# First mixing stage: one pair of transposes of the keys moved from TensorE to DMA, with the merge on ScalarE, and two scale vectors folded into one column

## The reference

```python
u = rmsnorm(h, mix_norm[l])
qa, ka, va, qb, kb, vb, qi, ki, wi, g = jnp.split(u @ w_in[l], SPLIT_POINTS, axis=-1)
qa = rmsnorm(qa.reshape(B, S, 8, 64), q_norm_dsa[l]);  ka = rmsnorm(..., k_norm_dsa[l])
qb = rmsnorm(qb.reshape(B, S, 8, 64), q_norm_moba[l]); kb = rmsnorm(..., k_norm_moba[l])
out_a = dsa_attention(qa, ka, va, qi, ki, wi, bias_dsa)    # only the 64 best keys of each query
out_b = moba_attention(qb, kb, vb, bias_moba)              # one block of 256: plain causal attention
g_a, g_b = jnp.split(sigmoid(g + b_gate[l]), 2, axis=-1)
h = h + (g_a * (out_a @ w_branch_dsa[l]) + g_b * (out_b @ w_branch_moba[l])) @ w_out[l]
```

## Time and profile before

| | |
|---|---|
| median of 3 runs | 997.86 us |
| the profiled execution | 998.35 us |
| its span, first to last instruction | 996.5 us |
| PE busy | 990.7 us, 99% |
| DVE busy | 689.2 us, 69% |
| ACT busy | 548.2 us, 55% |
| POOL busy | 116.0 us, 12% |
| granted TensorE clock | 1.0 of full speed throughout |

### The profile page before, as it was taken

The page is one execution under the profiler, slowest core; times in us unless marked ns, Lnnn a source line. Parts: engine busy times, 40 slices in busy tenths (PEclk is TensorE's granted clock), DMA queues, the critical chain, the costliest instruction groups (busy, mean ns, idle before and its releaser), DMA issues.

```text
span 996.5 us, 12586 instructions
## 1 busy us (share of the span) xinstructions
PE 990.7 (99%) x4632; PEld 813.2 (82%) x4632; DVE 689.2 (69%) x1010; ACT 548.2 (55%) x752; POOL 116.0 (12%) x109
## 2 busy tenths in 40 slices
PE   8999999999999999999999999999999999999998
PEld 7788888888877788888888888888888888888887
DVE  6756566668987667656566677797689767656663
ACT  7344443576765546444443576768875555443542
POOL 0000000022300000000000041168914000000000
DMA  7987776585444446666666376457556546787761
GB/s 258 283 262 258 234 253 211 185 307 175 147 150 141 169 133 211 227 204 208 220 195 226 127 259 211 141 177 211 148 183 199 205 152 212 227 221 227 223 199 43
DMA packets 159129, 199.87 MB, mean 201 GB/s; under 512 B 49633, under 2 KB 105322, under 8 KB 158954
## 3 DMA queue, kind: packets, MB, share of 16 engines
q1 hardware_dynamic: 159066, 199.24, 62.8%
q10 hardware_dynamic: 16, 0.00, 0.0%
HBM read 182.45 MB, written 5.77 MB: 189 GB/s over the span
## 4 chain that ended last, share of the span: by engine, by line
PE 97%; DVE 1%; DMA 1%; ACT 0%; SPq 0%; issue 0%; POOL 0%; ACTq 0%; DVEq 0%; POOLq 0%
PE bank L1902 23%; PE bank L1904 23%; PE bank L1903 23%; PE bank L2018 7%; PE bank L2019 7%; PE bank L2020 7%; PE bank L1917 1%; PE bank L2069 1%; PE bank L2183 1%; DMA halves_t<-halves 0%; DMA raw<-in_ffn_w_gu 0%; PE bank L2084 0%; PE bank L2071 0%; PE bank L2257 0%; PE bank L2141 0%; PE bank L2304 0%
## 5 line engine op out<-in xcount | busy, mean ns | idle before, releaser
L1902 PE MATMUL bank<-hi,xh 128*128 128x512 f32 (+1 forms) x944 | 375.2, 397 | 0.9 <-DVE lo L1520 0.8
L1904 PE MATMUL bank<-hi,xl 128*128 128x512 f32 (+1 forms) x944 | 367.4, 389 | 0.0
L1903 PE MATMUL bank<-lo,xh 128*128 128x512 f32 (+1 forms) x944 | 366.5, 388 | 0.0
L1277 DVE TENSOR_TENSOR lo<-raw,hi 128x2048 fp32r<-128x2048 f32 (+1 forms) x111 | 253.9, 2289 | 146.3 <-ACT hi L799 146.3
L799 ACT ACTIVATE hi<-raw 128x2048 fp32r<-128x2048 f32 (+1 forms) x114 | 216.5, 1901 | 132.3 <-PE bank L2020 96.9
L1902 PEld LDWEIGHTS bank<-hi,xh 128*128 128x128 f32 x944 | 177.3, 188 | 39.5 <-issue 3.1
L1904 PEld LDWEIGHTS bank<-hi,xl 128*128 128x128 f32 x944 | 177.2, 188 | 37.5
L1903 PEld LDWEIGHTS bank<-lo,xh 128*128 128x128 f32 x944 | 177.6, 188 | 34.2
L1294 DVE TENSOR_TENSOR lo<-raw,hi 128x1024 fp32r<-128x1024 f32 (+1 forms) x108 | 133.2, 1244 | 40.1 <-ACT hi L808 39.2
L2018 PE MATMUL bank<-hi,hh 128*128 128x512 f32 (+1 forms) x306 | 119.3, 390 | 0.4 <-DVE hl L1353 0.4
L2020 PE MATMUL bank<-hi,hl 128*128 128x512 f32 (+1 forms) x306 | 118.7, 388 | 0.0
(11 more groups left out here) (266 smaller groups left out, 963.2 us busy)
## 6 DMA issues: line engine op xcount, KB each, us to landing
raw<-in_w_in SPq DMA_DIRECT2D x48, 1024.0 KB
raw<-in_ffn_w_gu SPq DMA_DIRECT2D x82, 512.0 KB
raw<-in_ffn_w_down SPq DMA_DIRECT2D x22, 1024.0 KB
raw<-in_w_up SPq DMA_DIRECT2D x16, 1024.0 KB
raw<-in_w_down SPq DMA_DIRECT2D x16, 1024.0 KB
raw<-in_w_out SPq DMA_DIRECT2D x8, 1024.0 KB
distance_table<-ftab SPq DMA_DIRECT2D x8, 576.0 KB
raw<-in_w_proj_attn SPq DMA_DIRECT2D x4, 1024.0 KB
```

What stands on the lines that cost most here:

```text
L1277: nc.vector.tensor_tensor(lo[s][:, :, 0:width], raw[s][:, :, 0:width], hi[s][:, :, 0:width].bitcast(F32), ALU.subtract).then_inc(lo_done, 1)
L1902: nc.tensor.matmul(o, sh, wh, start=first and j == 0, stop=False)
L1903: nc.tensor.matmul(o, sh, wl, start=False, stop=False)
L1904: ins = nc.tensor.matmul(o, sl, wh, start=False, stop=last and j == 3)
```

## The change

The keys of group 2 (k_m) are no longer turned by PE. `M1_T` loses its two entries for group 2. Instead ACT writes the two 16-bit planes of `hid[:, t]` at steps 14 and 15; SP issues one DMA transpose for each t, placed in its order behind both loads of group 5 (units 10 and 11) and ahead of unit 12; ACT merges both turned halves into k_m with one instruction at step 17; and PE waits for that merge before the first scores (step 21). The planes and their turned form lie in `gates1[:, 0]`, which holds nothing at that time. The scale by the gain is not applied to k_m any more: a fifth DVE instruction in `constants` multiplies the column for q_m by the one for k_m, and q_m's eviction applies the product. The semaphores of the first feed-forward layer are used on. The pieces below are, in this order: the tables, the two views of gates1, SP's loop behind the two loads of group c, three pieces of ACT's loop (what a step does behind the split, the new instructions, the wait ahead of the eviction to hid), DVE's constants, and PE's first scores.

```diff
-M1_T = {(0, 0): 6, (0, 1): 7, (1, 0): 9, (1, 1): 10, (2, 0): 13, (2, 1): 14,
-        (4, 0): 21, (4, 1): 22, (5, 0): 25, (5, 1): 26}
+M1_T = {(0, 0): 6, (0, 1): 7, (1, 0): 9, (1, 1): 10, (4, 0): 21, (4, 1): 22, (5, 0): 25, (5, 1): 26}
+M1_PLANES = (14, 15)
+M1_MERGE = 17
...
+        m_planes = gates1[:, 0, 0:2 * W].bitcast(U16).rearrange("p (t c) -> p t c", t=NT)
+        m_turned_planes = gates1[:, 0, 2 * W:4 * W].bitcast(U16).rearrange("p (k c) -> p k c", c=SEQ)
...
+                if c == 5:
+                    for t in range(NT):
+                        sp_eng.wait_ge(ffns[0].planes, 2 * (NF1 - 1) + t + 1)
+                        sp_eng.dma_start_transpose(m_turned_planes[:, :, t * P:(t + 1) * P],
+                                                   m_planes[:, t, :]).then_inc(ffns[0].flip[t], 16)
...
-                        dst = {1: q_m, 2: k_m, 4: q_a, 5: k_a}[cc]
-                        g = {1: 2, 2: 3, 4: 0, 5: 1}[cc]
+                        dst = {1: q_m, 4: q_a, 5: k_a}[cc]
+                        g = {1: 2, 4: 0, 5: 1}[cc]
                         if order == 2:
-                            act.wait_ge(cols_done, 3)
+                            act.wait_ge(cols_done, 5)
...
+                if p in M1_PLANES:
+                    tt = M1_PLANES.index(p)
+                    act.wait_ge(m_qn, 2 + tt + 1)
+                    nc.scalar.activation(m_planes[:, tt, :].rearrange("p (s c) -> p s c", s=2),
+                                         hid[:, tt, :].bitcast(U16).rearrange("p (c s) -> p s c", s=2),
+                                         ACT.Copy).then_inc(ffns[0].planes, 1)
+                if p == M1_MERGE:
+                    for tt in range(NT):
+                        act.wait_ge(ffns[0].flip[tt], 16 * NF1)
+                    nc.scalar.activation(k_m[:, :, :].bitcast(U16).rearrange("p k (c s) -> p s k c", s=2),
+                                         m_turned_planes.rearrange("p (s k) c -> p s k c", s=2),
+                                         ACT.Copy).then_inc(ffns[0].merged, 1)
...
-                        if m >= 2:
-
-                            act.wait_ge(m_tr, m + 1)
+                        if c == 2:
+
+                            act.wait_ge(m_tr, 2 + t + 1)
+                        elif c == 4:
+                            act.wait_ge(ffns[0].planes, 2 * (NF1 - 1) + t + 1)
+                        elif c == 5:
+                            act.wait_ge(m_tr, 4 + t + 1)
...
+                dve.wait_ge(cols_done, 4)
+                g = C_GAIN + 2
+                nc.vector.tensor_tensor(cols[:, g:g + 1], cols[:, g:g + 1], cols[:, g + 1:g + 2],
+                                        ALU.mult).then_inc(cols_done, 1)
...
-                        pe.wait_ge(m_trev, 6)
+                        pe.wait_ge(m_trev, 4)
+                        pe.wait_ge(ffns[0].merged, NF1)
                     else:
                         pe.wait_ge(m_l, k)
                     if k == NH:
-                        pe.wait_ge(m_trev, 10)
+                        pe.wait_ge(m_trev, 8)
```

## The result

| | before | after |
|---|---|---|
| median | 997.80 us | 999.63 us |
| span of the profiled execution | 996.5 us | 997.7 us |
| that execution's own time | 998.35 us | 999.50 us |

The ratio is 1.0019, with an interval of 1.0012 to 1.0026: slower by 1.83 us (by the interval 1.2 to 2.6). The forecast was 997.6 in a range of 996.7 to 999.0, so the time lies outside it, by 0.6 us on the slow side. It is 0.18% and thus still within what I had called no change, but that is luck of the bound: the sign was wrong. Of the 16 executions of after one took 5704.57 us, for a reason that nothing here shows; it is left out of the ratio, and without it the median would be 999.60.

What follows compares the result with a forecast made beforehand. PE was taken to bound the kernel (97% of the chain), running little ahead of a saturated VectorE. Transposes -0.96, wait at step 23 +0.56, VectorE's delay +0.1 gave -0.3 us: 997.86 to 997.6, range 996.7 to 999.0.

Steps and rivals of the forecast that it cites:

- the rule of the prediction: PE's gain at step 23 is cut to 0.40 - d: transposes free 0.96 us, 0.56 + d returns as a wait.
- d: VectorE's delay at the head sums of step 18: landing - 243.0, range -0.18 to +1.3 us, passed on to PE.
- Landing: When both DMA transposes, issued behind unit 11's load, have arrived for ScalarE's merge: 243.1, range 242.5 to 244.3.
- rival B: Slower: the merge holds ScalarE's queue at step 17, and VectorE; from landing 243.4 on, +0.9 us at 244.3; chance 0.22.
- The sum: Whole kernel: -0.96 (transposes) + 0.56 (wait at step 23) + 0.1 (VectorE's delay) = -0.3 us, median to 997.6.
- -0.96 for eight transposes: PE at steps 13 and 14: removing two groups of four transposes frees 0.48 us each, up to 0.96 us.
- The cap: PE's scores at step 23 need VectorE's negated maximum, whose 0.40 us of slack limits the gain from the 0.96 freed.
- rival A: Full gain: transposes land by 242 or VectorE's slack at step 23 is larger; -0.96 us, 996.9; chance 0.19.
- SyncE's queue: The two transposes' issue makes unit 12's load late by 0 to 0.2 us, with five us of cover: no price.
- Edits without a price: Extra VectorE multiply in constants, product as q's scale, PE's merge wait at step 21, planes in gates1: no cost.

Runs made afterwards that it cites:

- e8: Changed kernel with the eight transposes put back on PE at steps 13 and 14, result unused: 999.83 against 997.96 us, 1.0018.
- e9: Changed kernel with SyncE holding unit 12's load back until both DMA transposes have landed: 999.56 against 997.96 us, 1.0017.
- e10: Changed kernel with the step 17 merge split into two instructions, one per t, each behind its own landing: 998.48 against 997.96 us, 1.0004.
- e7: Changed kernel with the merge at step 18 instead of 17: 997.76 against 997.96 us, 0.9997.
- e1: Changed kernel with the merge at step 19 instead of 17: 996.79 against 997.74 us, 0.9990.
- e2: Changed kernel with the step 17 merge reading unturned planes, the DMA transposes awaited only at step 21: 996.81 against 997.74 us, 0.9990.
- e3: Changed kernel with no transposes on any engine; ScalarE copies unturned keys to k_m at steps 14 and 15: 996.85 against 997.74 us, 0.9991.
- e4: Changed kernel with both DMA transposes ahead of unit 11's load instead of behind it: 996.93 against 997.74 us, 0.9991.
- e11: e1 with the top-k's last instruction moved from step 21 to 24 and the mask work two steps later: 996.54 against 997.96 us, 0.9985.
- e6: e1 with VectorE taking the logits of heads 1 and 3 one step earlier, with heads 0 and 2: 997.35 against 997.96 us, 0.9994.
- e5: Kernel before with only the folded scale (product of two gains as q's scale, k_m evicted with 1.0): 997.91 against 997.96 us, 1.0000.

## Why the prediction was wrong

The table sets the rule of the prediction, net = d - 0.40 at step 23, beside every run with a wait there (us; the last column against the executions of before taken with the run):

| | H | d | S | net measured | d - 0.41 | median against before |
|---|---|---|---|---|---|---|
| after | 17.43 | +2.44 | 31.12 | +2.03 | +2.03 | +1.83 |
| e8 | 17.48 | +2.49 | 31.18 | +2.09 | +2.08 | +1.87 |
| e9 | 17.35 | +2.36 | 31.04 | +1.95 | +1.95 | +1.60 |
| e10 | 16.09 | +1.10 | 29.79 | +0.70 | +0.69 | +0.52 |
| e7 | 15.64 | +0.65 | 29.34 | +0.25 | +0.24 | -0.20 |
| e1, e2, e3 | 14.73 | -0.26 | 28.41 | -0.68 | -0.67 | -0.95, -0.93, -0.89 |
| e4 | 14.74 | -0.25 | 28.42 | -0.67 | -0.66 | -0.81 |

Point by point:

- *The mechanism and the rule were right.* Landing, then merge, then hi, eviction and square in ScalarE's order, then VectorE without a gap, then PE at step 23. The slack read as 0.46 less 0.06 came out as 0.40 to 0.42 us in nine runs. e7 shows that VectorE carries it.
- *The step that failed is "Landing".* I took 243.1, range 242.5 to 244.3. It came at 236.50 + 7.99 = 244.49, in the clock of before 245.06: 2.0 us behind what I took and 0.8 beyond my end. The second transpose took 8.0 us of its own where the four second halves of the earlier trace rows had taken 4.0 to 5.9. I had used the second halves of the second mixing stage as a bound though they go out 2.4 to 3.7 us behind their load (the prediction says 3.1 to 3.7, which holds for the two slow ones) and this one 1.7. The first halves there, 0.5 us behind their load, took 6.1 to 7.6, and I left them out. I had seen the difference in distance and counted it as a reason against rival B; e4 and e9 show that a load just ahead is what delays them, so it spoke for B. Counted from the load's issue the landing took 9.7 us (244.49 - 234.77), near the 9.0 of the earlier trace rows; the forecast went wrong where it averaged that count, at its median, with the transposes' own delays.
- *The merge was mis-sized too.* 2.54 us measured (2.52 to 2.54 in all runs) against 1.9 taken and 2.1 as the upper bound. Twice the planes' 1.04 is not the price of a copy that writes interleaved 16-bit elements: half of it takes 1.37 (e10). That is +0.64 in d.
- *The sum.* d = 2.0 (landing) + 0.6 (merge) + the 0.1 already taken = 2.7, less 0.26 because neighbours on ScalarE overlap (2.39 from the merge's start to that of hi though it lasts 2.54, 1.88 from there to the eviction though hi lasts 1.99), is 2.44, as measured. With it the rule gives +2.03 instead of -0.3.
- *-0.96 for eight transposes was right*, shown by e11 and by e6 at step 23. The 2.2 us that eight times the 271 ns of one would give are more than twice that. Portions 13 and 14 now take 2.73 and 2.72 us, with no transposes in them.
- *The cap was right*: where the square of step 18 waits for no landing (e1 to e4) the gain in the stage stops at 0.68, which is 0.41 and the 0.26 by which the head sums could come earlier (I had allowed 0.18). That limit is why rival A fails too; its -0.96 in the stage is only to be had with e11's edit. The end times of e1 to e4 (-0.81 to -0.95) are nearly A's price all the same, by the difference that is left open below.
- *SyncE's queue:* unit 12 was 1.06 late instead of 0 to 0.2, as the second issue took 4.42 and not at most 3.47 us. It cost nothing, as said.
- *Edits without a price:* confirmed by e5. *The Trainium skill's rule of transposing DMAs as fast as plain ones* ("Advanced Engine Details and Errata", X-Bar Transpose): landing at 242 by it. The trace does not bear it out, though no run has a plain copy of the same data beside them: alone on the DMA engines the transposes of e4 moved 277 GB/s (236.4 to 237.3), unit 11's load in the kernel before 403 (238.2 to 239.4). That is small beside what decided: e4, where nothing is ahead of them, lands at 236.7 + 2.7 = 239.4, and the 6.9 and 8.0 behind a load are not in the rule.
- *Rival B was the right one* in place, price and point of decision (landing from 243.4 on). I gave it 0.22 up to a landing at 245.4 and +2, and its own arithmetic at 245.06 with a merge of 2.54 gives 2.06 + 0.64 - 0.40 = +2.3 (+2.03 with the overlap). The range ended at its row-bound 244.3; landing and merge both lay beyond the rows that I had used, in the same direction.
- *Not foreseen:* PE's wait of 1.55 us for a bank of the accumulators at step 20. By e7 and e8 it adds nothing; PE would have lost as much three steps later.

Open: why a transpose 1.7 us behind a 1 MB load takes 8.0 us and not 5.9, and what it does in the 1.8 us after its data have moved (e9). The distance to the load may be it: 6.1 to 7.6 us at 0.5, 4.0 to 5.9 at 2.4 to 3.7; but among the latter four the order does not follow the distance, and of it I varied only the sign, in e4. And most changed variants end 0.1 to 0.45 us lower against before than their stamp at step 23 says (last two columns; e11 0.45), also those with the transposes on PE or with none. PE's small waits for lo of other stages add up to anything from 0 to 1.4 us in one profiled run or another, which hides differences of that size; I have not found a cause.

## What to carry to other kernels

A wait placed in an in-order queue costs what stands behind it: at steps 17, 18 and 19 the same merge gave +1.83, -0.20 and -0.95 us against before, so put a wait on a DMA behind what a saturated engine needs next, and count the landing of a transfer behind a load from the load's issue, with rows of a similar distance as the bounds. A saving on the bounding engine counts only up to the slack of the engine that feeds it (0.68 of 0.96 here), and the rest was got by moving work that the bounding engine does not wait for behind what it does (e11). Pulling work forward (e6) lost more one step later than it gained. Where a small transfer and a big load are ready together and the load has slack, send the small one first (e4).

## What the runs showed of the hardware

- Two 256 KB transposing DMAs took 2.7 us each from issue to landing with nothing ahead of them (e4), and 6.9 and 8.0 us when they were issued 0.4 and 1.7 us behind a load of 1 MB (after; 6.8 to 8.5 in all eight runs of this order); the issue of the second held the queue for 4.42 instead of 1.23 to 1.25 us.
- Behind a load such a transpose landed 1.8 us after the DMA engines had moved their last data (e9: 242.7 and 244.5), with nothing ahead some 0.5 us after it (e4).
- A ScalarE copy of 16-bit elements took 1.04 us at 128x1024 when it read them interleaved and wrote them in runs (planes) and 1.37 when it read them in runs and wrote them interleaved (e10's merges); 2.54 at 128x2048, where an fp32 split of as many elements takes 1.91.
- Matmul rows overlap: 0.39 us long and 0.23 apart, so a bracket of idle time understates a hole by 0.16.
